# A two-layer trunk with expert retrieval: first part rebuilt, a second-layer modulation block moved behind the second part's projections

## The reference, cut to what matters

```python
mod = (c_act @ w_ada[l] + b_ada[l])[:, None, :]
sh1, sc1, g1, sh2, sc2, g2 = jnp.split(mod, 6, axis=-1)
h = rms_norm(x) * (1.0 + sc1) + sh1
proj = h @ w_in[l]
...
attn = dsa_attention(q, k, v, qi, ki, wi).reshape(B, T, ATTN_WIDTH)
conv = conformer_conv(cu, conv_dw[l], conv_b[l], conv_ln_g[l], conv_ln_b[l])
mixed = jnp.concatenate([rms_norm(attn, out_g_attn[l]), rms_norm(conv, out_g_conv[l])], axis=-1)
x = x + g1 * (mixed @ w_out[l])
h2 = rms_norm(x) * (1.0 + sc2) + sh2
x = x + g2 * peer_ffn(h2, peer_wq[l], peer_sub_keys[l], peer_u[l], peer_v[l])
```

## Time and profile before

| | |
|---|---|
| median of 3 runs | 1902.33 us |
| the three runs | 1896.08, 1902.33, 1903.36 us |
| span of the profiled execution, first to last instruction | 1733.4 us |
| the profiled execution's own device time | not listed; the median less the span is 168.9 us |
| busy: PE, DVE, POOL, ACT | 60%, 64%, 59%, 16% of the span |
| moved by DMA | 691.98 MB, 399 GB/s over the span |

### The profile page before, as it was taken

One profiled execution on the slowest core, in us unless ns is written; L12 is line 12 of the kernel. 1 busy time (PEld: TensorE's weight loads), 2 busy tenths in 40 slices (PEclk: granted clock), 3 DMA queues, 4 the chain that ended last, 5 costly groups with the idle time before them and its releaser, 6 DMA issues.

```text
span 1733.4 us, 18207 instructions
## 1 busy us (share of the span) xinstructions
PE 1039.2 (60%) x6158; PEld 590.6 (34%) x6158; DVE 1103.2 (64%) x3003; ACT 273.4 (16%) x717; POOL 1015.9 (59%) x1133
## 2 busy tenths in 40 slices
PE   7979897406896588603788569611689610005555
PEld 4547674303363156301345146500236200001111
DVE  1987989996218576888117676889513979991000
ACT  2141235202110035300101024400210100000000
POOL 2610435676655763566755664567655777776774
PEclk8989899657998799655899679765899865557888
DMA  9998999999999999999999999999999999999998
GB/s 373 393 368 327 405 405 383 409 409 409 409 409 407 408 404 410 397 410 397 410 409 409 394 409 408 399 407 409 406 406 402 391 410 410 409 410 389 409 409 330
DMA packets 195481, 691.98 MB, mean 399 GB/s; under 512 B 21360, under 2 KB 21376, under 8 KB 195134
## 3 DMA queue, kind: packets, MB, share of 16 engines
q0 software_dynamic: 147840, 537.06, 78.1%
q1 hardware_dynamic: 47550, 153.77, 22.8%
HBM read 689.71 MB, written 1.05 MB: 398 GB/s over the span
## 4 chain that ended last, share of the span: by engine, by line
DMA 41%; PE 24%; DVE 15%; POOL 13%; issue 6%; ACT 1%; SPq 0%; DVEq 0%; ACTq 0%; POOLq 0%
DMA rows<-in_peer_v,v_at 20%; DMA rows<-in_peer_u,u_at 18%; PE ps L921 8%; DVE rows L1586 8%; PE ps L876 7%; POOL rows L698 7%; POOL rows L690 6%; DMA kiw<-in_w_in 1%; PE ps L818 1%; PE ps L864 1%; PE ps L848 1%; DMA rows<-in_w_ada 1%; DVE rows L1568 1%; PE ps L735 1%; PE ps L804 1%
## 5 line engine op out<-in xcount | busy, mean ns | idle before, releaser
L690 POOL DMA_INDIRECT rows<-in_peer_u,u_at x512 | 482.5, 942 | 370.8 <-DVE dots L1586 202.5
L1586 DVE CUSTOM_DVE_ANT_0 rows<-rows,ps 128x1024 f32<-128x1024 f32 x512 | 610.3, 1219 | 92.5 <-DMA rows<-in_peer_u,u_at 78.6
L698 POOL DMA_INDIRECT rows<-in_peer_v,v_at x512 | 485.7, 949 | 283.9 <-PE ps L921 153.4
L921 PE MATMUL ps<-rows,spread_c 128*32 128x512 f32 x2048 | 325.7, 764 | 215.0 <-DMA rows<-in_peer_v,v_at 215.0
L735 PE MATMUL ps<-ident 128*128 128x128 f32 x228 | 39.9, 346 | 354.3 <-DVE dots L1586 354.3
L921 PEld LDWEIGHTS ps<-rows,spread_c 128*32 128x32 f32 x2048 | 71.4, 125 | 414.8 <-issue 412.6
L735 PEld LDWEIGHTS ps<-ident 128*128 128x128 f32 x228 | 35.6, 183 | 369.8 <-DVE dots L1586 356.6
L876 PEld LDWEIGHTS ps<-hT,wring 128*128 128x128 f32 x1152 | 137.0, 199 | 25.7 <-issue 24.1
L876 PE MATMUL ps<-hT,wring 128*128 128x128 f32 x1152 | 142.2, 285 | 0.0
L848 PE MATMUL ps<-wring,hT 128*128 128x512 f32 x256 | 117.1, 600 | 8.3 <-DMA wring<-in_w_in 7.5
L902 PE MATMUL ps<-diag_eq,hc 128*128 128x128 f32 x744 | 104.7, 307 | 25.3 <-ACT diag_eq L1274 25.2
(11 more groups left out here) (254 smaller groups left out, 1183.9 us busy)
## 6 DMA issues: line engine op xcount, KB each, us to landing
wring<-in_w_in SPq DMA_DIRECT2D x34, 1024.0 KB, 13.2
wring<-in_w_ada SPq DMA_DIRECT2D x31, 1024.0 KB, 10.6
wring<-in_peer_wq SPq DMA_DIRECT2D x28, 1024.0 KB, 9.6
rows<-in_w_ada SPq DMA_DIRECT2D x16, 1024.0 KB, 14.9
wring<-in_w_out SPq DMA_DIRECT2D x13, 1024.0 KB, 17.1
rows<-in_peer_u,u_at POOLq DMA_INDIRECT x512, 14.1
rows<-in_peer_v,v_at POOLq DMA_INDIRECT x512, 9.5
rows<-in_w_in SPq DMA_DIRECT2D x6, 1024.0 KB, 15.9
```

The costliest lines, as they stand in the source:

```text
L690: pool.indirect_dma_start(row(n), None, u_rows, bass.IndirectOffsetOnAxis(ap=u_at[:, p % 2, k:k + 1], axis=0)).then_inc(row_landed[n % SLO ...
L698: pool.indirect_dma_start(row(n), None, v_rows, bass.IndirectOffsetOnAxis(ap=v_at[:, p % 2, tok:tok + 1], axis=0)).then_inc(row_landed[n % ...
L921: ins = pe.matmul(ps[32 * g:32 * g + 32, YB + q, :], spread_c[:, g, a, :], row(n)[:, q * 512:q * 512 + 512], start=a == 0, stop=a == 31)
L1586: dve.tensor_tensor_reduce(out=row(n), in0=row(n), in1=h2_shown, scale=1.0, scalar=0.0, op0=ALU.mult, op1=ALU.add, accum_out=dots[:, k:k + ...
```

## The change

The computation is the same and so are the bytes. What moves:

- In the modulation table, layer-2 products leave the places ahead of routing, except `product(1, 0)`, which goes to "mix". `product(0, 3)` and `turn(0, 2)` go up to "conv". `product(1, 1)` stands behind routing block 1, `product(1, 3)` behind block 2, `product(1, 4)` in "tail", behind part 1's projections. None stands behind block 0.
- The v projection of part 0 goes from ahead of the logits to behind them; `lnB` (`spread_ln`) goes the other way.
- The convolution's channel group 0 goes from DVE to PE (`conv_first`), with 31 diagonal tiles made by ACT in `g1`, `g2` and `skT`; DVE keeps 62 steps, all ahead of the logits. PE's transposes of groups 1 to 3 stand behind v.
- The sub-keys' turns and copies go from "mix" to just ahead of `h2T`, and their load in SP's order from ahead of `("ada", 0, 3)` to ahead of `("wq", 0, 0)`.
- `("wq", 0, 0)` is loaded in two halves by columns, so that routing block 0's first half needs the first piece alone.
- DVE makes half of the first `hT`; `turn(0, 0)` goes ahead of `product(0, 1)`; some `stay_busy` go.

```diff
-TAP_STEPS = (24, 18, 25)
+TAP_STEPS = (24, 18, 20)
...
     (0, "pre"): [product(0, 0)],
-    (0, "pre2"): [product(0, 1)],
-    (0, "preT"): [turn(0, 0), turn(0, 1)],
-    (0, "conv"): [product(1, 0), product(1, 1)],
-    (0, "S"): [turn(1, 0), turn(1, 1)],
-    (0, "mix"): [turn(0, 2), product(0, 3)],
-    (0, "out"): [turn(0, 3), turn(0, 4)],
-    (0, "wq0"): [product(1, 3)],
-    (0, "wq1"): [product(1, 4)],
-    (0, "wq3"): [turn(1, 3), turn(1, 4)],
-    (0, "tail"): [product(0, 5), turn(0, 5)],
+    (0, "pre2"): [turn(0, 0), product(0, 1)],
+    (0, "preT"): [turn(0, 1)],
+    (0, "conv"): [product(0, 3), turn(0, 2)],
+    (0, "S"): [turn(0, 3)],
+    (0, "mix"): [product(1, 0)],
+    (0, "out"): [turn(0, 4)],
+    (0, "wq1"): [turn(1, 0), product(1, 1)],
+    (0, "wq2"): [product(1, 3)],
+    (0, "wq3"): [turn(1, 1), turn(1, 3)],
+    (0, "tail"): [product(1, 4), turn(1, 4), product(0, 5), turn(0, 5)],
...
+SLOTS_OF = {("ada", 0, 3): (4, 5, 6, 7), ("out", 0, 0): (8, 3), ("ada", 1, 0): (DIAG_SLOT, 0, 1, 2),
+            ("adav", 0, 4): (4, 5, 6, 7), ("out", 0, 1): (LATE_SLOT, DIAG_SLOT), ("sk", 0): (0,), ("wq", 0, 0): (1, 2),
+            ("wq", 0, 1): (4, 5), ("ada", 1, 1): (6, 3, DIAG_SLOT, 0), ("wq", 0, 2): (1, 2),
+            ("ada", 1, 3): (3, 4, DIAG_SLOT, 0), ("wq", 0, 3): (1, 2)}
...
+            def conv_first():
+
+                o = ps[:, CONV_BANK, 0:P]
+                pe.wait_ge(consts_made, 1)
+                pe.wait_ge(glu_done, 1)
+                pe.matmul(o, ident[0:TAPS + 1, TAPS:TAPS + 1].to_broadcast([TAPS + 1, P]), cw_raw[0:TAPS + 1, 0:P],
+                          start=True, stop=False)
+                for i in range(TAPS):
+                    if i % 8 == 0:
+                        pe.wait_ge(first_diag_ready, i // 8 + 1)
+                    pe.matmul(o, hc[:, 0, i:i + P], first_diag(i), start=False, stop=i == TAPS - 1)
...
                     proj(("k", p), hT)
-                    proj(("v", p), hT)
+                    spread_ln(l)
+                    conv_first()
                     ada(p, "conv")
...
-                    spread_ln(l)
+                    proj(("v", p), hT)
+                    pe.wait_ge(conv_dve, CT - 2)
+                    pe.wait_ge(conv_pool, 1)
+                    for ct in range(1, CT):
+                        ins = pe.transpose(ps[:, CONV_BANK, ct * P:(ct + 1) * P], acc[:, ct, :], ident[:, :])
+                    ins.then_inc(conv_full, 1)
                     ada(p, "S")
...
                 if p == 0:
-                    stay_busy(10)
+                    subkey_turns(p)
+                    stay_busy(4)
                 pe.wait_ge(h2_ready, p + 1)
...
-            tap_steps = [(i, ct) for i in range(TAPS) for ct in range(CT - 1)]
+            tap_steps = [(i, ct) for i in range(TAPS) for ct in range(1, CT - 1)]
...
                 for n in CHUNKS[t]:
                     logits(n)
-                if p == 0:
-                    taps(len(tap_steps))
                 conv_norm(p)
```

More of the change, by code:

```diff
@@ L189, in plan @@
                 job("dot", l, n)
-            for name in ("k", "v"):
-                both(name, p)
+            both("k", p)
+            for i in range(2):
+                job("lnB", l, i)
             ada(p, "conv")
@@ L213, in plan @@
         if p == 0:
-            for i in range(2):
-                job("lnB", l, i)
+            both("v", p)
             ada(p, "S")
@@ L517, in wait_weight_used @@
             name = uses[i][0]
-            if uses[i] in vec_count:
+            if uses[i] == (("wq", 0, 0), 0):
+                b, n = bank(("qp", 0, 0, 0))
+                eng.wait_ge(full[b], n)
+            elif uses[i] in vec_count:
                 eng.wait_ge(ada_taken, vec_count[uses[i]])
@@ L558, in tap_diag, with first_diag @@
             return diags[:, n % 2, j, :]
+        def first_diag(i):
+            if i < 16:
+                return (g1 if i < 8 else g2)[:, (i % 8) * P:(i % 8 + 1) * P]
+            return skT[:, i - 16, :]
         def batches_to(p, n):
@@ L633, in _ @@
                 else:
-                    w = weight_slot(slot).rearrange("p (k n) -> p k n", k=2 if name[0] in WIDE else 4)
+                    rows_each = 2 if name[0] in WIDE else KT if name == ("wq", 0, 0) else 4
+                    w = weight_slot(slot).rearrange("p (k n) -> p k n", k=rows_each)
                     src = source(name, h)
@@ L824, in proj_heads @@
             def proj_heads(block, rhs, between):
-                w = [piece(block, 0), piece(block, 1)]
                 for c, name in enumerate(jobs_of(block)):
@@ L829, in proj_heads @@
                         between()
+                    w = piece(block, c, KT)
                     b, o = open_job(*name)
@@ L1001, in project, with subkey_turns @@
                 conv(p, 5)
+            def subkey_turns(p):
+                raw = piece(("sk", p), 0, 16)
+                for n in range(4):
+                    turn4(("skT", p, n), [raw[:, 4 * n + i, :] for i in range(4)])
+            def conv_first():
[8 more added lines that the diff above has]
+                    pe.matmul(o, hc[:, 0, i:i + P], first_diag(i), start=False, stop=i == TAPS - 1)
             def first(p):
@@ L1028, in first @@
                 ada(p, "preT")
-                def subkey_turns():
-                    raw = piece(("sk", p), 0, 16)
-                    for n in range(4):
-                        turn4(("skT", p, n), [raw[:, 4 * n + i, :] for i in range(4)])
                 def index_dots():
@@ L1364, in first @@
                     act.sem_inc(cw_ready, 1)
-                    ada(p, "pre2")
-                    ada(p, "preT")
                     act.wait_ge(rope_args, 1)
@@ L1369, in first @@
                     act.activation(flat, flat, ACT.Sin).then_inc(rope_ready, 1)
+                    ada(p, "pre2")
+                    ada(p, "preT")
+                    act.sem_inc(first_mod_ready, 1)
                 if p != 1:
@@ L1372, in first @@
                 if p == 0:
+                    for i in range(TAPS):
+                        ins = act.activation(first_diag(i), ident[:, :], ACT.Copy, scale=cwT[:, 0, i:i + 1])
+                        if i % 8 == 7 or i == TAPS - 1:
+                            ins.then_inc(first_diag_ready, 1)
                     sigmoid(p)
@@ L1427, in attend @@
                 if p == 0:
-                    copy_ln(l)
+                    seq_(act.activation(rsum[:, 0:1], ident[:, 0:1], ACT.Exp))
+                    for n in ns:
+                        exponentials(n)
+                    evac(("v", p), vals[:, t, :], proj_ready)
                     ada(p, "S")
                     for n in ns:
-                        exponentials(n)
-                    for n in ns:
                         turned_out(n)
-                    copy_subkeys(p)
                 else:
@@ L1947, in _ @@
             take_y(PARTS - 1)
-STAGE_PLACES = [(p, where) for p in range(PARTS) for where in ("pre", "pre2", "preT", "conv", "S", "mix", "out", "wq0", "wq1", "wq3", "tail")]
+STAGE_PLACES = [(p, where) for p in range(PARTS) for where in ("pre", "pre2", "preT", "conv", "S", "mix", "out", "wq0", "wq1", "wq2", "wq3", "tail")]
 _INS = ["x", "c", "positions", "w_ada", "b_ada", "w_in", "q_norm_g", "k_norm_g", "idx_k_ln_g",
```

43 lines of the change are left out of this document (21 added, 22 removed).

## The result

| | before | after |
|---|---|---|
| median (fastest to slowest) | 1903.44 us (1896.08 to 1909.19) | 1920.61 us (1903.98 to 1926.67) |
| executions | 8 | 8 |
| profiled execution: time, span | - | 1923.61, 1921.4 us |

The ratio is 1.0079 (95% interval 1.0051 to 1.0108): **slower by 15 us** (10 to 21), beyond the 7 us forecast and outside the range.

A forecast was written before the change was run, and what follows sets the result against it. DMA was taken to bound the kernel: lost time up to the gathers grows from 19.0 to 26.3 us (+7.3), giving 1740.7 us span plus 168.9 around it, 1909.6 us. Range 1900 to 1918 us.

The forecast's parts named there:

- 410 GB/s at a busy share of 1.03 ... these losses are the reader's map: Whole kernel: all bytes at 410 GB/s take 1687.8 of 1733.4 us; the other 45.6 us are lost DMA time.
- The bytes up to the first gather: Loads ahead of the gathers: 51 pieces asked for instead of 56, 54.9 MB in all, worth 134.0 us of DMA.
- plus 168.9 around it: Final sum: 168.9 us around the span, added to a span of 1740.7 us.
- `product(1, 4)` in the tail adds the bytes there that it takes from ahead: Behind part 1's projections: four pieces moved to the tail, no further loss after the first gather.
- The chain: Engine events from the start to the first gather: it is issued at 158.7 us, 9.5 us earlier.
- The output projection's clock term: PE idles some 3 us ahead of the output projection; lower clock costs 1.0 us, bounds nothing or 2.5.
- v as what `conv_norm` waits for: Attention, part 0: PE's v sets conv_full at 104.0 us, so conv_norm begins at 104.1, 11.0 us earlier.
- ACT as the narrow place: Ahead of routing: ACT's sub-key copies, 4.48 us, delay its half of h2T to 141.1 us; 0.3 us given back.
- B: Rival: the engines' chain decides, not the bytes; the whole program shifts 9.5 to 10.5 us earlier, 1892 us; chance 0.10.
- A: Main case: lost DMA time grows by 2 to 12 us, likeliest 1909.6 us; chance 0.70.
- C: Rival: routing starves behind the sixth gather, row 6 waiting for product(1, 3) beyond 183 us; 1917.1 us; chance 0.14.
- a rival by which PE never falls: PE's clock stays full if busy from 36 to 112 us; block 0 about 1 us earlier, 1908.6 us; no chance given.

The follow-up runs named there:

- base trace: The first profiled execution of the kernel before, used for the prediction; span 1733.4 us, where the timed median is 1903.44 us.
- e2_eT: The changed kernel with PE's turn of the expert numbers and ACT's gate Exp moved ahead of the tail's products; 0.9996 of the kernel before.
- e2_all: The changed kernel with the expert numbers' turn ahead of the tail and product(1, 3) moved to the tail too; 1.0006 of the kernel before.
- second trace of before: The kernel before, unchanged, run and profiled again among the experiments; ratio 0.9994.
- e1_defer: The kernel before with only product(1, 4) and its turn moved to the tail; 1.0062 of the kernel before.
- e2_defer_eT: The kernel before with product(1, 4) in the tail and the expert numbers' turn ahead of the tail; 0.9987 of the kernel before.
- e3_ahead: e2_eT with 300 dummy transposes on PE just ahead of the expert numbers' turn; 1.0115 of the kernel before.
- e2_warm: The changed kernel with 22 dummy transposes on PE behind product(1, 0); 1.0058 of the kernel before.
- e3_behind: e2_eT with 300 dummy transposes on PE behind the expert numbers' turn and the tail's products; 1.0160 of the kernel before.

## Why the prediction was wrong

By its own steps:

- **"410 GB/s at a busy share of 1.03 ... these losses are the reader's map" failed.** The base trace ran at 406 GB/s behind 310 us, typical executions at 370. With 10% of room by the rate (6% by the busy share, 0.97 against 1.03), 7 MB that come late can come later at no cost. The bytes up to the first gather were counted well (54.9 MB; the trace has 55.3 by 170 us), but the gathers came 8.6 us later than forecast, so that the lost time up to 170 us was 35.2 us (170 less 55.3 / 0.410) against 19.0, **16 us more and not 7.3**. By the prediction's own rule this gives almost exactly the 15 us measured, and that agreement is luck: `e2_eT` has 5.3 MB less by 170 us, `e2_all` 6.6, and neither has a loss.
- **"plus 168.9 around it" failed.** It is 2.2 us. A gap of 9% between a span and a median was a sign that the trace was of another kind of execution, and I explained it away instead of distrusting the rates.
- **"`product(1, 4)` in the tail adds the bytes there that it takes from ahead", cost nothing, failed.** It is the step that carries the result. I counted its transfers and not what stands behind it in PE's order: `eT`, `v_at`, part 1's first jobs and, through ACT's order, the GELU. The base trace did not warn of it. There PE turned the numbers at 294.09 us and DVE copied them, without a wait, at 327.95 (rows below this list): 34 us of cover. In the second trace of before it is 13 (337.55 to 350.68), and the product in the tail made `eT` 31 us later. Cost shown: 0.62% alone (`e1_defer`), and the whole of it back with `eT` moved (`e2_eT`, `e2_defer_eT`).
- **The chain, 9.5 us forecast and 0.9 measured.** The first projection ended at 53.9 us (the next starts there, PE row above), 2.1 later than in the base trace (51.8) instead of 1.0 earlier: it began 0.8 later, and its first 32 records took 6.63 us where the next 32 took 3.74 (5.36 and 3.74 in the base trace). `conv_first` is 62 records, 3.84 + 3.51 us, not 32: the trace has two records for each f32 matmul, so that its "x32" and "x30" are the 16 and 15 of the program's order. Four matmuls of k (eight records) took 5.40 where 3.60 is the full clock. These three add up to 8.4 us, of which 6.3 reached `conv_full`. The output projection's clock term was 3.1 us (6.70 against 3.60), beyond the bound of 2.5 and 2.1 more than the 1.0 taken. 6.3 and 2.1 are nearly all of the 8.6 us by which the first gather missed its forecast.
- **Right:** v as what `conv_norm` waits for; ACT as the narrow place (its half of `hT` ended at 150.8 us, 0.8 behind DVE's); gaps from 140 us on (88 GB/s from 140 to 145 us, 11 from 150 to 155), though they last to 170 (30 from 165); and the count of bytes. The sign came out too, but by another mechanism than the one forecast.
- **The rivals.** B, "the chain decides", is as wrong as A: the first gather's time shows nowhere (`e2_eT` issued it 5.5 us ahead of before, at an equal time). C had the right shape, a wait in order on DVE with work queued behind it, and the wrong place: not routing at 183 us but `finish_choice` at 355.

The base trace's rows for the third point, PE and DVE:

```profile
294.09 0.27 PE L729 MATMUL ps<-ident,expert 128*128 128x128 f32 x1
```
```profile
327.95 0.29 DVE L1869 CAST v_at<-ps 128x128 uint32<-128x128 f32 x1
```

The Trainium skill (TensorE: Matmul & The Clock Gate, "Part 1: The HAM clock gate") had been weighed as a rival by which PE never falls. The trace shows it fell: after a pause of 3.75 us ahead of a turn (the `mT` turn at 121.95 us), the first four matmuls of the output projection took 6.70 us, at a granted clock of 0.50 from 125 to 130 us. That fits a clock that follows how busy PE has been, and not the rival's premise that PE would not pause.

**What stays open.** How the loss divides between the wait at `v_at` and ACT's GELU. In `e3_ahead` the two are 16.3 and 10.9 us over `e2_eT`; in after they are 13.9 and 3.7 over before. Moving `eT` with the Exp shortened both, and no run moved the GELU alone. How the late `coef` turns into the final time is read from the correlation only. Why the base trace ran at 406 GB/s is open too; none of the thirteen later profiles shows it.

## What to carry to other kernels

When work is moved to a place where "the data is late anyway", ask first what stands behind it in the engine's own order, and follow that through the next engine's order as well: here PE's product delayed DVE's copy and, by ACT's queue, DVE's coefficients. A transfer-bound product belongs behind the small job that others wait for; here that exchange was worth 12 us on one chip (`e2_warm` against `e2_eT`) and 15 against the change as first timed. And compare a trace's span with the timed median before its rates are used as a ceiling.

## What the runs showed of the hardware

**PE can stall with nothing to wait for while the DMA engines are full.** The dummies of `e3_behind` wait for nothing. The first 160 ran at 0.12 us each. Then (PE):

```profile
359.96 19.19 PE L750 MATMUL ps<-ident 128*128 128x128 f32 x160
379.36 0.27 PE L750 MATMUL ps<-ident 128*128 128x128 f32 x1 [0.22 <-issue]
...
410.22 0.37 PE L750 MATMUL ps<-ident 128*128 128x128 f32 x1 [2.43 <-issue]
413.02 0.37 PE L750 MATMUL ps<-ident 128*128 128x128 f32 x1 [2.43 <-issue]
415.83 0.37 PE L750 MATMUL ps<-ident 128*128 128x128 f32 x1 [2.44 <-issue]
...
434.81 13.11 PE L750 MATMUL ps<-ident 128*128 128x128 f32 x103 [0.34 <-issue]
```

Single transposes, 0.7 to 2.8 us apart, from 379 to 434 us, while DMA is full, and the remaining 103 in 13 us as soon as it is not:

```profile
380.00:434.00 54.00, 12.43 (x35) 6.22 (x36) 45.05 (x74) 0.00 (x0) 35.73 (x38) 0.53 1.03 409
434.00:448.00 14.00, 13.56 (x107) 13.20 (x107) 0.00 (x0) 0.00 (x0) 0.00 (x0) 0.85 0.48 191
```

A full DMA alone did not stop them at once: it carried 408 to 409 GB/s from 360 us on, while the first 160 ran at their rate. In `e3_ahead` the same 300 dummies took 38 us in place of 88. DMA carried 258 to 340 GB/s during its first 195; they then paused for 3.5 us, and the last 98 ran in 12.5 us with DMA at 170 GB/s and less.

The profile's page lists two queues of instructions among the DMA queues (`e3_behind`: packets, MB, share):

```profile
q8 instruction: 52, 0.85, 0.2%
q14 instruction: 42, 0.34, 0.1%
```

Instructions thus come over the same DMA engines. That they are what PE lacked is argued, not shown by a run of its own. Such "issue" pauses make 16% of the chain of waits of after and 13% in the second trace of before, but 18% in `e2_eT`, which has no loss: they are not what made the change slower. PE work placed where DMA is full can so take far longer than its rows elsewhere say: 0.12 us a transpose by the first row, 1.5 us on average in the 54 us.
